# Forty instead of twenty-eight expert rows looked up in the first of two output passes of a mixture-of-experts layer, one core

## The reference

```python
def block(args):
    xt, it, gt = args
    u = expert_u[it]
    pre = jnp.einsum('tkd,td->tk', u, xt, preferred_element_type=jnp.float32)
    act = (jax.nn.gelu(pre, approximate=False) * gt).astype(xt.dtype)
    return jnp.einsum('tk,tkd->td', act, expert_v[it])
```

## Time and profile before

| what | value |
|---|---|
| median of 3 runs | 3954.95 us (3952.35 to 3970.26) |
| the profiled execution | 4004.14 us, span 4002.5 us |
| PE busy | 3715.4 us, 93% of the span |
| DVE busy | 2686.2 us, 67% |
| GpSimd busy | 1950.8 us, 49% |
| granted PE clock, mean of the span | 0.969 |

### The profile page before, as it was taken

One profiled execution on the slowest core, in us unless ns is written; L12 is line 12 of the kernel. 1 busy time (PEld: TensorE's weight loads), 2 busy tenths in 40 slices (PEclk: granted clock), 3 DMA queues, 4 the chain that ended last, 5 costly groups with the idle time before them and its releaser, 6 DMA issues.

```text
span 4002.5 us, 54934 instructions
## 1 busy us (share of the span) xinstructions
PE 3715.4 (93%) x19212; PEld 3173.4 (79%) x19212; DVE 2686.2 (67%) x5194; ACT 1246.6 (31%) x1825; POOL 1950.8 (49%) x1352
## 2 busy tenths in 40 slices
PE   8988789999898899999999999999789999899999
PEld 6854478888677678899999999999668888677777
DVE  5443377776322437748888887887796666688887
ACT  3013233433211321233333333333333333333333
POOL 1023113222100016888888888888888888221210
PEclk9989889999999999999999999999889999999999
DMA  3259300000320024478888888887889998899997
GB/s 114 101 196 399 146 19 9 18 9 10 105 90 26 27 105 92 71 199 263 267 271 266 262 251 268 261 264 202 245 219 283 276 279 219 321 369 366 355 370 267
DMA packets 376223, 788.61 MB, mean 197 GB/s; under 512 B 136992, under 2 KB 245536, under 8 KB 342176
## 3 DMA queue, kind: packets, MB, share of 16 engines
q1 hardware_dynamic: 210208, 451.28, 33.2%
q0 software_dynamic: 165888, 336.01, 28.6%
HBM read 643.09 MB, written 144.05 MB: 197 GB/s over the span
## 4 chain that ended last, share of the span: by engine, by line
PE 27%; POOL 16%; DMA 6%; issue 6%; DVE 6%; DVEq 2%; ACT 1%; SPq 1%; POOLq 0%; ACTq 0%
PE peer_ps L2159 13%; POOL gates_d L2049 12%; PE peer_ps L2068 9%; DMA peer_gat<-gates_d 5%; PE peer_ps L2082 4%; POOL rows L2037 2%; POOL peer_rows L2037 2%; DVE late_rows L2442 1%; DVEq L2456 1%; DVE peer_acc L2457 1%; DVEq L2372 1%; PE peer_ps L2105 1%; DMA late_in<-gates_d 1%; DVE late_in L2464 1%; ACT peer_vh L2253 0%
## 5 line engine op out<-in xcount | busy, mean ns | idle before, releaser
L2049 POOL DMA_INDIRECT gates_d<-peer_gates,peer_idx x768 | 1363.8, 1776 | 300.9 <-issue 222.5
L2068 PE MATMUL peer_ps<-high,peer_uh 128*128 128x384 f32 x2048 | 528.9, 339 | 37.9 <-DVE peer_ul L2359 31.9
L2068 PE MATMUL peer_ps<-low,peer_uh 128*128 128x384 f32 x2048 | 523.8, 336 | 0.0
L2068 PE MATMUL peer_ps<-high,peer_ul 128*128 128x384 f32 x2048 | 523.6, 336 | 0.0
L2068 PEld LDWEIGHTS peer_ps<-high,peer_uh 128*128 128x128 f32 x2048 | 370.8, 190 | 50.3 <-issue 43.1
L2159 PE MATMUL peer_ps<-peer_vh,peer_ah 128*128 128x512 f32 x1026 | 329.9, 403 | 53.7 <-DVE peer_al L2476 53.1
L2068 PEld LDWEIGHTS peer_ps<-low,peer_uh 128*128 128x128 f32 x2048 | 373.8, 190 | 0.0
L2068 PEld LDWEIGHTS peer_ps<-high,peer_ul 128*128 128x128 f32 x2048 | 373.1, 189 | 0.0
L2037 POOL DMA_INDIRECT late_rows<-in_expert_uv,peer_idx x108 | 140.2, 1298 | 429.3 <-DVE peer_acc L2457 381.5
L2159 PE MATMUL peer_ps<-peer_vh,peer_al 128*128 128x512 f32 x1026 | 322.5, 396 | 0.0
L2159 PE MATMUL peer_ps<-peer_vl,peer_ah 128*128 128x512 f32 x1026 | 321.5, 395 | 0.0
(11 more groups left out here) (477 smaller groups left out, 7745.8 us busy)
## 6 DMA issues: line engine op xcount, KB each, us to landing
late_in<-in_expert_uv SPq DMA_DIRECT2D x170, 512.0 KB, 5.5
gates_d<-mla_zeros POOLq DMA_DIRECT2D x128, 512.0 KB, 30.1
hidden_d<-peer_hid SPq DMA_DIRECT2D x128, 384.0 KB, 3.5
peer_raw<-in_expert_u SPq DMA_DIRECT2D x86, 512.0 KB, 5.2
peer_val<-in_expert_uv SPq DMA_DIRECT2D x86, 512.0 KB
late_in<-hidden_d SPq DMA_DIRECT2D x170, 192.0 KB, 6.6
late_in<-gates_d SPq DMA_DIRECT2D x170, 192.0 KB, 7.1
first_raw<-in_expert_u SPq DMA_DIRECT2D x42, 512.0 KB, 5.3
```

The lines of the kernel that those rows point to most:

```text
L2049: pool.indirect_dma_start(gates_flat, bass.IndirectOffsetOnAxis(ap=idx[:, n, k:k + 1], axis=0), gates[:, n, k:k + 1], None, compute_op=ALU ...
L2068: last = nc.tensor.matmul(ps[i][:, a, 0:HD], w[:, cols], x[:, kc, a * HD:(a + 1) * HD], start=(kc == 0 and w is uh[i % 2] and x is high), ...
```

## The change

Forty instead of 28 lookups go into the first pass, so 68 instead of 80 into the second. In the first pass DVE meets a group of two in every sixth slot instead of every eight and a half, and in the second in every three and a half instead of every third. The dot products of the first pass's groups now stand at q = 13, 19, 25, 31, 37 and so on to 127; they stood at 13, 21, 30, 38, 47 to 123. Nothing is added or taken away in total.

```diff
-EARLY_SLOTS, PASS_SLOTS = 148, 28
+EARLY_SLOTS, PASS_SLOTS = 148, 40
...
             g -= EARLY_SLOTS // GROUP
-            return OUT + 13 + (g * 17) // 2 if g < PASS_SLOTS // GROUP else OUT + NK + 3 + 3 * (g - PASS_SLOTS // GROUP)
+            return OUT + 13 + 6 * g if g < PASS_SLOTS // GROUP else OUT + NK + 3 + (7 * (g - PASS_SLOTS // GROUP)) // 2
```

## The result

| | before | after |
|---|---|---|
| median | 3967.11 us | 4034.07 us |
| lowest and highest of 6 runs | 3952.35, 3980.88 | 4015.27, 4045.87 |
| ratio to before, 95% interval | | 1.0157 [1.0131, 1.0183] |
| profiled execution | 4004.14 us | 4015.27 us |

The change makes the kernel 1.6% slower, about 62 us (0.0157 x 3967). The forecast of 3972 us and its range are too low. The two profiled executions are only 11 us apart: before's, at 4004 us, is longer than all six of its runs, and after's, at 4015, is the shortest of its six. The median of before was 3955 us over the three runs that the forecast stood on and is 3967 over six, so 12 of the 62 us between 3972 and 4034 are the starting value.

A forecast was written before the change was run, and what follows sets the result against it. It took scatters on GpSimd to open the second pass and the DMA engines to bound it; last scatter +46, gates -3, second pass -26 gave +17 on 3955, so 3972 us, 8-in-10 range 3940 to 3998.

The forecast's parts named there:

- 1. Twelve lookups: GpSimd's list ahead of the last scatter: twelve more lookups at 1.63 us each, nothing hiding them, +19.5 us.
- 2. Buffer waits: First pass: GpSimd waits for DVE's sums ahead of three lookups (m = 8, 10, 12), about +24 us.
- 3. DVE slows GpSimd: First pass: DVE's extra work lengthens scatters by 6 us, the last ones gain about 4; taken as +2.5 us.
- 4. Fewer lookups beside the gates: At the seam: four instead of six lookups share the DMA engines with the first gates, -3 us.
- 5. The second pass: Second pass: lower DMA demand per block brings back 26 of 32.5 us lost against PE's pace, -26 us.
- The second pass stays late: Rival, 17%: pairs of lookups still delay gates whatever their spacing; only 10 us come back, 3988 us.
- GpSimd hardly waits: Rival, 19%: in the first pass the slot count is off or DVE further ahead; -7 us, 3948 us.
- The seam is covered: Rival, 10%: unprofiled GpSimd's last scatter lands well before SP asks; only part 5 counts, about -26, 3929 us.

The follow-up runs named there:

- nowait: The kernel after, with the first pass's lookups begun one unit (16 scatters) later so that none waits for a buffer: 3995.63 us, 1.0062 of before.
- fewer: Before with twelve lookups left out altogether, 28 in the first pass and 68 in the second at the change's 3.5-block spacing: 1.0036 of before.
- a1: The changed kernel measured and profiled again, no edit: 4021.05 us, 1.0130 of before; second pass 547.9 us.
- none2: Before without any lookup in the second pass, 80 left out: 0.9939 of before; second pass 518.2 us.
- b2: The kernel before, profiled once more without edit; no timed ratio; second pass 526.8 us.
- b1: The kernel before measured and profiled again, no edit: 3967.88 us, 1.0000 of before; second pass 558.1 us.
- fewer4: Before with twenty lookups left out, 60 in the second pass in groups evenly four blocks apart: 1.0058 of before; second pass 551.8 us.

## Why the prediction was wrong, by its own steps

*1. Twelve lookups, +19.5 us.* Right: +18.0 us at the seam (nowait against fewer), 15.4 timed.

*2. Buffer waits, +24 us.* Right in place and nearly in size: 8.4, 13.9 and 6.3 us where 5, 13 and 5.5 were worked out, 28.6 together. Taking them away gave 21.7 us at the seam and 25.4 timed. Some of the 28.6 comes back because GpSimd's later scatters are shorter in after, as the next part shows.

*3. DVE slows GpSimd, +2.5 us.* The wrong sign: last scatter +38.9 less about 20 of lookups less 28.6 of waits leaves about -10. The mean of a scatter fell from 1816 to 1780 ns (250 x 0.036 = 9 us). Nearly all of it lies in the last 32 scatters: 1.63 us each where they took 1.86. They run while DVE has nothing to do and, from 3393 us on, PE neither: 1.54 us each, as in the timeline above. The prediction had allowed 4 us for this, against 6 for DVE's extra work. The Trainium skill (GPSIMD Engine Reference, section 8 Key points) says that GpSimd contends with VectorE's instructions of two SBUF inputs. The trace agrees in kind (1.54 us with DVE idle, 1.85 beside its work), though PE stands at that time too and the DMA share is 0.23 (3382 to 3422 us), and here it worked as a relief. So the seam came to +39.7 us against the +43 of parts 1 to 4.

*4. Fewer lookups beside the gates, -3 us.* Didn't come: 13.62 against 13.44 us, and 31.0 instead of 30.3 us from last scatter to second pass. Leaving all of them away does help (4.70, 5.58 us), so four lookups delay the gates as much as six.

*5. The second pass, -26 us.* This is the step that failed; it gave nothing back. It failed in two ways.
- The 32.5 us lost were read from one execution with a long second pass. The same kernel takes 526.8 to 558.1 us there. From the timed runs the usual length can be estimated: a1 is 53 us above before, 39.7 of that is the seam, so before's usual pass is about 13 us shorter than after's 547, some 534 us. There was about 16 us to win over none2's 518, not 32.5. The estimate takes the rest of the kernel to be equally long in both.
- "The DMA engines bound that pass" was wrong. I had taken the packets' share of the time (0.97) over their number as a price of a lookup, 2.71 us, and of a block, 2.53. (The 67.11 MB are 64 lookups' rows, not 66, so the first should have been 2.79.) But b2 moves 388 GB/s at a share of 1.01 with PE waiting 1.9 us, and b1 362 at 0.98 with 21.2. Nor is the price fixed: without any lookup none2's block takes 3.05 us of packets (74.7% of 440 us over 107.9 blocks), beside them b2's takes 2.48 (59.7% over 106.1) and before's 2.53. The clearest case is fewer4: by an estimate from the sizes of its loads it asks at PE's own pace for 5.77 MB in 16.3 us, 354 GB/s. That is less than b2 moved, and still its pass is 25 us longer than b2's. The Trainium skill (DMA: Bandwidth & Descriptors, section Where 436 GB/s comes from) puts what HBM gives one core at about 358 GB/s, a stack's rate divided by two cores, which I took as fitting my 359. Here one core is at work, and its 388 GB/s over 440 us show that this share was no bound. What the trace of fewer4 points to instead is the burst: a pair of lookups, 2 MB, ahead of the next gates. The change made the bursts fewer, and took away the one spacing at which they could cost little.

*The rivals.* "The second pass stays late" (17%) was nearest to what happened, at 3988 us; it fails too, for it still gave 10 us to the new spacing, where the timed runs take 12. "GpSimd hardly waits" falls with the three waits. "The seam is covered" falls by the timed runs: with GpSimd 20 us ahead of the trace, the waits (25.4 us) and the twelve lookups (15.4 us) could not both have cost what they did.

*The sum.* Timed: 25.4 + 15.4 + 12.3 = 53 us on that chip. The forecast was +17. Of the 36 us between, 38 are part 5 (-26 against +12), and -2 the seam. In the result the change cost 62 to 67 us; how the 9 to 14 us more split isn't known, and the intervals of the two measurements, 1.0131 to 1.0183 and 1.0096 to 1.0165, overlap.

*What stays open.* Why a spacing of three blocks can be cheap while 3.5, 4 and 4/2 were not, and what makes before's second pass short or long, isn't settled. A link of the first with the three load buffers fits the spacings run, but was only argued: no kernel with four buffers was tried. The chip is a rival for the second, since b1 and b2 ran on different ones, but an estimate speaks against it. The "in" part ended between 2788.5 and 2813.5 us in all profiles, before's second pass started some 625 us later, and its executions ended 11 us behind the pass. If the timed executions kept to these, the shortest of before on b1's chip, 3954.68 us, leaves at most 530 us for the second pass, and the longest, 3995.14 us, at least 546. So by this estimate the executions of before on one chip had short passes and long ones. How often each comes can't be seen, since those executions left no trace.

## What to carry to other kernels

Before a gain is worked out from time lost in one profile, take that profile twice more and compare the loss with the timed runs: here the stage varied by 31 us in unchanged code, more than the 26 us that the change was to bring in it. Then bound the gain from above by leaving the work out altogether, which showed with one kernel that all 80 lookups are worth some 24 us. And when bursts of gathers run beside a ring of loads, their spacing against the number of buffers can matter more than their number: try the spacing by itself.

## What the runs showed of the hardware

- One core moved 388 GB/s over 440 us (b2), at a summed packet share of 1.01 over the 16 DMA engines, while the same code in another execution moved 359 at 0.97. Without lookups a block's packets took 3.05 us in the sum (none2), with them 2.48 to 2.53 (b2, before). In these runs a share near 1 didn't tell a saturated stretch from one with room.
- Unchanged code took 526.8 us for one stage in one execution and 558.0 and 558.1 in two others, with the granted clock at 1.00 in each; the "in" part, the same code in all kernels here, ended anywhere from 2788.5 to 2813.5 us.
- A scatter took 1.54 us on GpSimd with DVE idle (the last ones of after), and 1.854 on average beside its work.
- The first gates of the second pass (192 KB) took 4.70 us alone, 5.58 with the lookups held back, and 13.4 to 13.6 us with four or six lookups of 1 MB issued beside them.
